# Norm affine and modulation applied to turned rows, bare normalised rows gathered, router by strips, opening reordered

## Chip, cores and metric

One core of a Trainium2 chip. The metric is device microseconds (us) of one execution of the whole program; lower is better. A core has TensorE (PE; its weight loads are listed as PEld), VectorE (DVE), ScalarE (ACT), GpSimd (POOL), SyncE (SP) and 16 DMA engines. The engines run their own instruction lists and meet at semaphores. A row of the trace names the line of the kernel that wrote the instruction.

## What is computed

A two-layer encoder in float32, 256 tokens of 1024 features, one conditioning vector c. Every sub-layer is modulated by vectors that come from c (`w_ada`), and closed by a layer norm with gain and offset:

```python
x = layer_norm(ALPHA * x + (1 + g1) * y, ln_mix_g[l], ln_mix_b[l])
h = x * (1 + sc2) + sh2
y = grouped_moe(h, router_w, router_b, w_gate[l], w_up[l], w_down[l])
x = layer_norm(ALPHA * x + (1 + g2) * y, ln_ffn_g[l], ln_ffn_b[l])
```

Layer 0's mixer is a causal convolution of 31 taps between two projections, layer 1's an attention with a forget gate (its keys and values have a modulation of their own, `w_ada_kv`). `grouped_moe` takes a softmax over 16 experts for each token, picks the best of four groups by the sum of its two best, and gives the token to those two experts.

## The kernel before

Tokens lie on the partitions in two tiles of 128 (`xs` for x, `hs` for h or for y). A product contracts over partitions, so h is turned: `turn_h` (L792) makes 16 transposes into PSUM banks 0 to 3, and `copy_hT` copies the banks to `hT` (ACT two, L552, DVE two, L1213).

Vectors that act along features are rows. `spread_row` (L767) multiplies a row by ones, which fills two PSUM banks with copies of it; DVE then combines all of `xs` with them. A close (`close_sublayer`) scales y by the gate row (L1271), adds it to x (L1275), takes mean and variance (L1280, L1283), normalises (L1288), multiplies by the gain row and adds the offset row (L1235, four operations). `modulate` does the same with scale and shift into `hs` (L1253, L1258); it also puts the features in the order in which the weights lie, a stride of four floats. PE spreads one row after another as DVE lets the banks go (`norm_spreads`), and between them computes the next part of `c @ w_ada` (`ada`, L742; the operand is c copied 32 times, `crep`), which DVE adds to its bias (`add_ada`, L1221).

`moe`: PE computes the router's logits with `hT` as the stationary operand (L852), DVE ranks experts and groups in small linked steps (L1299 to L1301), PE counts tokens, DVE builds places. Then for each expert and each block of 32 slots: DVE builds a 0/1 matrix G; PE gathers token rows of `hs` with it (`sum_x`, L885) and turns them (`turn_x`, L895); DVE copies them to `XT` (`take_xT`, L1389); PE multiplies by gate and up weights (`strips`, L904), DVE multiplies the two (L1399), PE turns that; DVE builds the weighting matrix (L1381, L1385), PE turns it (L922), combines the block before (L932) and multiplies by the down weights. An expert with several blocks runs the hidden part for all of them, then the result part. `zero_sums` (L858) clears four banks by a product, since results are added there.

Weights come in loads of 2 MB into a ring of eight slots (SP, L399), each load waiting until PE has used what its slot held; in the experts the slots are passed on by POOL (L511), and a ninth slot opens when the logits are done. Small rows go by ACT's and POOL's queues: x, then `b_ada`, then the rows of the convolution (`colrows`, L536).

In the opening PE takes two pieces of `w_ada`, turns `colrows` (L985), spreads taps (L993), takes two more pieces, spreads two rows, turns h and runs the first projection (L1011). The taps run on DVE (L1480) and PE (L1040); then come the convolution's norm over partitions (L1054, L1495, L1060) and the second projection (L808).

## Time and profile before

| | us |
|---|---|
| median of 3 runs | 1455.3 (1451.65 to 1455.41) |
| profiled execution | 1454.18 |
| its span | 1452.4 |
| PE busy | 1157.3 (80%) |
| DVE busy | 411.1 (28%) |
| ACT busy | 170.9 (12%) |
| chain that ended last | PE 56%, DMA 31%, DVE 8%, ACT 2% |

The stages of the profiled execution: the opening to 52.8, layer 0's mixer to 179.7, its close and the router to 234.4, its experts to 706.5, a close to 729, keys, values and attention to 902, a close and the router to 952, the second layer's experts to 1434, the last close and the output to the end. Shares of busy time are averages over stages with different limits; what a change is worth in a stage is read from what ends the waits there, and from when a load may be issued. The strips of the page cut the span in 40 slices of 36.3 us.

### The profile page before, as it was taken

To read this page: it belongs to the slowest core of one execution; us is meant where nothing else is said; L and a number is where in the kernel's file an instruction comes from. 1 tells how busy PE (TensorE), PEld (TensorE's weight loads), DVE (VectorE), ACT (ScalarE), POOL (GpSimd) and SP (SyncE) were. 2 spreads that over 40 slices of the span, in tenths; PEclk is the share of its full clock that TensorE was granted. 3 is DMA by queue.
4 is the path that set the end of the run, shared out by engine and by line. 5 is a ranking of instruction groups with operands and counts; after the bars stand their busy time and mean duration, and the time that the engine had idled before them with its cause. 6 is when DMAs were issued, how large, how long until landed. Compare 5 with 4: busy or idle time off the path is not lost.

```text
span 1452.4 us, 30514 instructions
## 1 busy us (share of the span) xinstructions
PE 1157.3 (80%) x13016; PEld 662.2 (46%) x13016; DVE 411.1 (28%) x1293; ACT 170.9 (12%) x415; POOL 21.4 (1%) x58
## 2 busy tenths in 40 slices
PE   2799978767998669867789989787689997697675
PEld 1685444433555335433374763444255553354342
DVE  0597063111222112111621331622122222121115
ACT  0003110000111001000100331010011110010001
POOL 3100000000000000000000000000000000000000
PEclk7899968888999899989879999678899998899887
DMA  9809859999999999999964022769999689999980
GB/s 374 358 20 421 357 245 398 425 425 426 366 395 410 426 427 425 422 424 424 416 273 151 24 117 92 313 268 426 423 425 396 279 353 426 427 425 422 424 347 30
DMA packets 49282, 494.70 MB, mean 341 GB/s; under 512 B 4231, under 2 KB 4247, under 8 KB 8988
## 3 DMA queue, kind: packets, MB, share of 16 engines
q1 hardware_dynamic: 48176, 490.75, 81.3%
q10 hardware_dynamic: 684, 2.32, 0.4%
q8 instruction: 77, 1.26, 0.3%
q0 software_dynamic: 320, 0.16, 0.1%
q14 instruction: 25, 0.20, 0.0%
HBM read 492.17 MB, written 1.05 MB: 340 GB/s over the span
## 4 chain that ended last, share of the span: by engine, by line
PE 56%; DMA 31%; DVE 8%; ACT 2%; issue 2%; ACTq 0%; DVEq 0%; POOL 0%; POOLq 0%
PE PS L904 25%; DMA ring<-in_w_up_dram 17%; DMA ring<-in_w_gate_dram 13%; PE PS L808 6%; PE PS L1011 4%; PE PS L932 3%; PE PS L742 3%; PE PS L885 2%; PE PS L826 2%; PE PS L1111 2%; DMA work<-in_conv_ln_b_dram 2%; DVE work L1381 1%; PE PS L895 1%; DVE xs L1235 1%; PE PS L792 1%
## 5 line engine op out<-in xcount | busy, mean ns | idle before, releaser
L904 PE MATMUL PS<-ring,work 128*32 128x256 f32 x8064 | 524.3, 417 | 114.6 <-DMA ring<-in_w_gate_dram 53.0
L904 PEld LDWEIGHTS PS<-ring,work 128*32 128x32 f32 x8064 | 280.2, 119 | 349.0 <-issue 110.5
L1399 DVE TENSOR_TENSOR work<-work,PS 128x256 f32<-128x256 f32 x47 | 19.8, 421 | 540.1 <-PE PS L904 540.1
L808 PE MATMUL PS<-ring,work 128*128 128x512 f32 x192 | 83.1, 593 | 0.5 <-ACT work L695 0.5
L742 PE MATMUL PS<-ring,crep 128*32 128x512 f32 x448 | 60.0, 689 | 19.7 <-DVE crep L1445 11.3
L932 PE MATMUL PS<-work 32*128 32x256 f32 x784 | 73.1, 499 | 3.1 <-ACT work L599 1.0
L904 PE MATMUL PS<-work 128*32 128x256 f32 x960 | 63.2, 408 | 15.4 <-DMA work<-in_w_up_dram 15.4
L922 PE MATMUL PS<-ident,work 128*128 128x128 f32 x94 | 22.9, 329 | 64.1 <-DVE work L1385 64.1
L1480 DVE SCALAR_TENSOR_TENSOR work<-work,colv 128x256 f32<-128x256 f32 x150 | 64.2, 486 | 1.2
L885 PE MATMUL PS<-hs,work 128*32 128x256 f32 x784 | 56.3, 406 | 3.8 <-DVE work L1372 3.8
L808 PEld LDWEIGHTS PS<-ring,work 128*128 128x128 f32 x192 | 36.3, 190 | 46.1 <-issue 45.3
L1410 DVE COPY work<-PS 128x256 f32<-128x256 f32 x47 | 20.0, 425 | 129.2 <-PE PS L932 129.2
L1011 PE MATMUL PS<-work,ring 128*128 128x256 f32 x256 | 55.5, 379 | 0.8 <-DVE work L1213 0.8
L599 ACT ACTIVATE work<-PS 128x256 f32<-128x256 f32 x47 | 18.1, 384 | 322.8 <-PE PS L904 322.8
L585 ACT ACTIVATE work<-PS 128x256 f32<-128x256 f32 x49 | 18.8, 384 | 316.0 <-PE PS L885 316.0
L1381 DVE TENSOR_SCALAR work<-slots,late,share 128x128 f32<-128x128 f32 x188 | 52.3, 341 | 0.9 <-issue 0.9
L1011 PEld LDWEIGHTS PS<-work,ring 128*128 128x128 f32 x256 | 48.6, 190 | 7.6 <-DVE work L1213 1.0
L904 PEld LDWEIGHTS PS<-work 128*32 128x32 f32 x960 | 32.6, 116 | 41.5 <-DMA work<-in_w_up_dram 19.3
L932 PEld LDWEIGHTS PS<-work 32*128 32x128 f32 x784 | 43.4, 225 | 17.5 <-ACT work L599 7.7
L589 ACT ACTIVATE work<-PS 128x256 f32<-128x256 f32 x47 | 18.1, 384 | 240.9 <-PE PS L904 240.9
L922 PEld LDWEIGHTS PS<-ident,work 128*128 128x128 f32 x94 | 10.2, 152 | 77.9 <-DVE work L1385 71.7
L742 PEld LDWEIGHTS PS<-ring,crep 128*32 128x32 f32 x448 | 15.6, 123 | 58.4 <-issue 46.0
(220 smaller groups left out, 884.9 us busy)
## 6 DMA issues: line engine op xcount, KB each, us to landing
ring<-in_w_gate_dram SPq DMA_DIRECT2D x64, 2048.0 KB, 26.2
ring<-in_w_up_dram SPq DMA_DIRECT2D x54, 2048.0 KB, 26.2
ring<-in_w_down_dram SPq DMA_DIRECT2D x54, 2048.0 KB, 27.9
ring<-in_w_ada_dram SPq DMA_DIRECT2D x24, 2048.0 KB, 18.8
work<-in_w_up_dram SPq DMA_DIRECT2D x10, 2048.0 KB, 23.9
work<-in_w_down_dram SPq DMA_DIRECT2D x10, 2048.0 KB, 27.4
ring<-in_w_pw_dram SPq DMA_DIRECT2D x6, 2048.0 KB, 38.8
ring<-in_w_ada_kv_dram SPq DMA_DIRECT2D x4, 2048.0 KB, 15.1
```

Of the source, the lines that this page charges most:

```text
L742: last = pe.matmul(PS[32 * q:32 * q + 32, bank, :], crep[:, k, :], quarter(index + j, kk, 2)[:, q * BANK:(q + 1) * BANK], start=(k == 0), ...
L808: last = pe.matmul(PS[:, banks + 2 * t + q, :], rows[:, k, t * P:(t + 1) * P], quarter(index + h, kk, KH)[:, q * BANK:(q + 1) * BANK], sta ...
L826: last = pe.matmul(PS[:, banks + f // 2, (f % 2) * SEQ:(f % 2 + 1) * SEQ], quarter(index + h, kk, KH)[:, f * P:(f + 1) * P], hT[:, k, :], ...
L885: last = pe.matmul(X_ps[SLOTS * q:SLOTS * (q + 1), :], G[:, t, :], hs[:, t, q * QUART:(q + 1) * QUART], start=(t == 0), stop=(t == TT - 1) ...
L904: last = pe.matmul(dst[SLOTS * s:SLOTS * (s + 1), :], rows[:, cc, SLOTS * q:SLOTS * (q + 1)], quarter(load + h, kk, KH)[:, QUART * s:QUART ...
L922: last = pe.transpose(GWT_ps[:, t * P:(t + 1) * P], GW[0][:, t, :, :].rearrange("p r s -> p (r s)"), ident[:, :])
L932: last = pe.matmul(sums(t, s), GWT[SLOTS * s:SLOTS * (s + 1), t * P:(t + 1) * P], yb[SLOTS * s:SLOTS * (s + 1), :], start=False, stop=(clo ...
L1011: last = pe.matmul(PS[:, f, g * SEQ:(g + 1) * SEQ], quarter(L_PW1 + j, kk, 2)[:, g * D + f * P:g * D + (f + 1) * P], hT[:, k, :], start=(k ...
L1111: last = pe.matmul(PS[:, (i + 1) % 2, SEQ:2 * SEQ], quarter(L_WQ + k // KH, k % KH, KH)[:, i * P:(i + 1) * P], hT[:, k, :], start=(k == 0) ...
L1381: last = dve.tensor_scalar(GW[i][:, t, :, :], every, late[i][:, t:t + 1], share[i][:, t:t + 1], ALU.is_equal, ALU.mult)
L1410: dve.tensor_copy(GWT, GWT_ps).then_inc(GWT_copied, 1)
L1480: ins = dve.scalar_tensor_tensor(out=CV[:, fc, :], in0=U[:, fc, j:j + SEQ], scalar=colv[:, fc, j:j + 1], in1=CV[:, fc, :], op0=ALU.mult, o ...
```

## The change

Vectors along features become columns: `columns` multiplies the rows that hold a modulation by a few columns of the identity, so that each feature's value stands on its partition (`mcol`); the norm vectors are turned once in the opening (`lncol`). `affine` on POOL combines gain, offset, scale and shift to one pair of columns a stage (`acol`): n*g*s and b*s + t. After a close only n = (x - mean) * rstd is made, into `hs`, one tile on DVE and one on ACT; it is turned, and `copy_hT` applies the pair. `sum_x` gathers rows of n, and `take_xT` applies the pair to the gathered tokens. x itself (n*g + b) is made later by `keep_x`, during the first expert or the key projection. The logits are computed with `rw` as the stationary operand, four products abreast in strips of 32 partitions, the strips then summed by a second small product. The ranking compares all pairs at once. ACT clears the sums. c is broadcast instead of copied. In the opening x is turned before its modulation is known, small rows are issued in another order, and the columns of the convolution are turned and the taps spread later.

PE's list in the opening, from the last of the spread taps on (the rows ahead are L742 x16, L985 and the rest of L993), before:

```order
L993 MATMUL PS<-colv,ident 32x8x7
L742 MATMUL PS<-ring,crep 32x512 x16
L767 MATMUL PS<-modv,ones 128x512 x4
L792 MATMUL PS<-ident,hs 128x128 x16
L1011 MATMUL PS<-work,ring 128x256 x128
```

and after, from its start:

```order
L826 MATMUL PS<-ring,cact 32x512 x8
L886 MATMUL PS<-ident,xs 128x128 x16
L826 MATMUL PS<-ring,cact 32x512 x24
L862 MATMUL PS<-ident,modv 128x4 x4
L1090 MATMUL PS<-ident,work 128x36 x8
L1094 MATMUL PS<-ident,work 128x8 x8
L1117 MATMUL PS<-work,ring 128x256 x32
```

The turning (L792, now L886) moved from behind all of `w_ada` to behind its first piece; the projection (L1011, now L1117) follows the turned columns, and its first two eighths stand ahead of the taps.

PE's list from the last product of layer 0's mixer to the first counting product, before:

```order
L1070 MATMUL PS<-work,ones 128x512 x4
L767 MATMUL PS<-modv,ones 128x512 x2
L742 MATMUL PS<-ring,crep 32x512 x32
L767 MATMUL PS<-lnrows,ones 128x512 x4
L767 MATMUL PS<-modv,ones 128x512 x4
L792 MATMUL PS<-ident,hs 128x128 x16
L852 MATMUL PS<-rw,work 128x16 x16
L742 MATMUL PS<-ring,crep 32x512 x16
L868 MATMUL PS<-r_sel,before 128x16
```

and after:

```order
L1176 MATMUL PS<-work,ones 128x512 x4
L851 MATMUL PS<-modv,ones 128x512 x2
L862 MATMUL PS<-ident,modv 128x4 x8
L826 MATMUL PS<-ring,cact 32x512 x32
L886 MATMUL PS<-ident,hs 128x128 x16
L945 MATMUL PS<-work,rw 32x256 x8
L953 MATMUL PS<-lane,work 128x16 x4
L851 MATMUL PS<-lnrows,ones 128x512 x4
L826 MATMUL PS<-ring,cact 32x512 x16
L965 MATMUL PS<-r_sel,before 128x16
```

The broadcasts of `lnrows` went from ahead of the turning to behind the logits, those of `modv` before it gave way to eight products for columns, and the logits are 8 + 4 products for 16.

DVE's list in the loop over an expert's blocks, from the building of G (L1368 and L1372) on, before:

```order
L1368 TENSOR_SCALAR work<-slots,place 128x32 x2
L1370 REGISTER_ALU
L1372 SCALAR_TENSOR_TENSOR work<-slots,place,work 128x32 x2
L1399 TENSOR_TENSOR work<-work,PS 128x256
L1389 COPY work<-PS 128x256
```

and after:

```order
L1481 TENSOR_SCALAR work<-slots,place 128x32 x2
L1483 REGISTER_ALU
L1485 SCALAR_TENSOR_TENSOR work<-slots,place,work 128x32 x2
L1517 TENSOR_TENSOR work<-work,PS 128x256
L1505 TENSOR_TENSOR work<-PS,acol 128x256
L1507 TENSOR_TENSOR work<-work,acol 128x256
```

The copy of the gathered tokens became two operations.

The core of the diff:

```diff
             def load(index, source):
                 if index in opens:
-                    sp.wait_ge(logits_done, opens[index] + 1)
+                    sp.wait_ge(logits_parted, 2 * opens[index] + 2)
...
+            def affine(to, gain, offset, scale, shift):
+                pool.tensor_tensor(acol[:, to, 0, :], lncol[:, :, gain], mcol[:, scale[0], scale[1], :], ALU.mult).then_inc(acol_part, 1)
+                pool.tensor_tensor(acol[:, to, 1, :], lncol[:, :, offset], mcol[:, scale[0], scale[1], :], ALU.mult).then_inc(acol_part, 1)
+                parts_made[0] += 2
+                pool.wait_ge(acol_part, parts_made[0])
+                pool.tensor_tensor(acol[:, to, 1, :], acol[:, to, 1, :], mcol[:, shift[0], shift[1], :], ALU.add).then_inc(acol_ready, 1)
+            pool.wait_ge(lncol_copied, 1)
+            pool.wait_ge(col_copied, 2)
+            affine(OF_FFN0, MIX_G, MIX_B, (2, 0), (1, 1))
...
-            act.wait_ge(mods_zeroed, 3)
-            load_bias(modv[0], b_ada[0], 3, mod0_in)
...
+            act.wait_ge(mods_zeroed, 3)
+            load_bias(modv[0], b_ada[0], 3, mod0_in)
...
+            for r, w in ((MIX_G, ln_mix_g), (MIX_B, ln_mix_b), (FFN_G, ln_ffn_g), (FFN_B, ln_ffn_b)):
+                act.dma_start(brow[32 + r:32 + r + DEPTH, :], w).then_inc(lnr_in, 16)
...
+            def copy_hT(scale, shift, ready=None):
+                if ready is not None:
+                    act.wait_ge(acol_ready, ready)
                 for b in (0, 2):
                     act.wait_ge(h_turned, 4 * turned[0] + b + 1)
-                    act.activation(hT[:, 2 * b:2 * b + 2, :], PS[:, b, :].rearrange("p (k t) -> p k t", k=2),
-                                   ACT.Copy).then_inc(hT_copied, 1)
+                    for k in (2 * b, 2 * b + 1):
+                        last = act.activation(hT[:, k, :], PS[:, b, (k % 2) * SEQ:(k % 2 + 1) * SEQ], ACT.Identity,
+                                              bias=shift[:, k:k + 1], scale=scale[:, k:k + 1])
+                    last.then_inc(hT_copied, 1)
...
+                if norms[0] < 2 * TT * DEPTH:
+                    act.wait_ge(shift_ready, norms[0] // TT)
+                    act.activation(chunks(hs, 1), by_chunk(xs[:, 1, :]), ACT.Identity, bias=negm[:, 0:1],
+                                   scale=rstd[:, 1:2]).then_inc(n_half, 1)
...
+                for b in range(4):
+                    act.activation(PS[:, b, :], ones[:, 0:1].to_broadcast([P, BANK]), ACT.Copy,
+                                   scale=0.0).then_inc(sums_zeroed, 1)
...
+            def spread_mod(tile, v, bank):
...
+            def turn_n(norms):
+                pe.wait_ge(h_ready, norms)
+                pe.wait_ge(n_half, norms)
+                turn_h(lambda t, k: hs[:, t, k * P:(k + 1) * P])
...
+            def moe(index, l):
+                h_there()
+                for kk in range(2):
+                    for q in range(4):
+                        last = pe.matmul(PS[32 * q:32 * q + 32, (B_GATE, B_M)[kk], 0:SEQ],
+                                         rw[:, 2 * q:2 * q + 2, :].rearrange("p k e -> p (k e)"), hT[:, 2 * q + kk, :],
+                                         start=True, stop=True, tile_position=(0, 32 * q), skip_group_check=True)
+                    last.then_inc(logits_parted, 1)
+                pe.wait_ge(parts_kept, l + 1)
+                pe.wait_ge(parts_copied, l + 1)
+                for t in range(TT):
+                    for kk in range(2):
+                        last = pe.matmul(PS[:, B_UP, 2 * E + t * E:2 * E + (t + 1) * E],
+                                         parts[:, kk, t * P:(t + 1) * P], lane[:, kk * E:(kk + 1) * E],
+                                         start=(kk == 0), stop=(kk == 1))
+                last.then_inc(logits_done, 1)
                 pe.wait_ge(rows_in[l], ROWS)
-                spread_ln(2 * which)
-                spread_ln(2 * which + 1)
...
-                for t in range(TT):
-                    for k in range(KD):
-                        last = pe.matmul(PS[:, B_GATE, t * E:(t + 1) * E], hT[:, k, t * P:(t + 1) * P],
-                                         rw[:, k, :], start=(k == 0), stop=(k == KD - 1))
-                last.then_inc(logits_done, 1)
...
-                    for b in range(4):
-                        behind(pe.matmul(PS[:, b, :], ident[0:1, 1:2].to_broadcast([1, P]), hs[0:1, 0, 0:BANK],
-                                         start=True, stop=False, skip_group_check=True))
...
+                    if e == 0:
+                        pe.wait_ge(sums_zeroed, 4 * (l + 1))
...
+            pe.wait_ge(c_acted, 1)
+            ada_load(L_ADA0_G0, 0, 4)
             pe.wait_ge(consts, CONSTS)
-            pe.wait_ge(c_spread, 1)
-            ada_load(L_ADA0_G0, 0, 0)
-            ada_load(L_ADA0_G0, 1, 0)
+            pe.wait_ge(x_in, 16 * TT)
+            turn_h(lambda t, k: by_chunk(xs[:, t, :])[:, k // KH, k % KH, :])
+            for j in range(1, ADA_G):
+                ada_load(L_ADA0_G0, j, 4)
+            pe.wait_ge(ada_added, 1)
+            columns(5, ((modv[0], 0),))
...
+            pe.wait_ge(lnr_in, 16 * 4)
+            for k in range(KD):
+                last = pe.matmul(PS[:, 6, 384 + 8 * k:392 + 8 * k], by_chunk(brow[32:40, :])[:, k // KH, k % KH, :],
+                                 ident[32:40, 32:40], start=True, stop=True, tile_position=(32, 0), skip_group_check=True)
...
-            ada_load(L_ADA0_G0, 2, 0)
-            ada_load(L_ADA0_G0, 3, 0)
-            pe.wait_ge(ada_added, 1)
-            spread_mod(modv[0], 1)
-            spread_mod(modv[0], 0)
-            pe.wait_ge(taps_copied, 3)
-            turn_h()
...
+            h_there()
             for f in range(KD):
+                if f == 2:
+                    pe.wait_ge(cols_copied, 1)
+                    pe.wait_ge(lncol_copied, 1)
+                    for q in range(4):
+                        for s in range(4):
+                            of_shift = colv[:, :, s:TAPS:4]
+                            last = pe.matmul(PS[32 * s:32 * s + 32, 7, 64 * q:64 * (q + 1)].rearrange("p (k m) -> p k m", k=KD)[:, :, 0:of_shift.shape[2]],
+                                             ident[:, 32 * q:32 * q + 32], of_shift, start=True, stop=True,
+                                             tile_position=(0, 32 * s), skip_group_check=True)
...
             pe.wait_ge(ada_added, 3)
-            norm_spreads(0, 0, L_ADAKV)
+            spread_mod(modv[0], 2, 4)
+            columns(7, ((modv[0], 1), (modv[0], 2)))
+            ada(L_ADAKV, 6)
+            turn_n(1)
             pe.wait_ge(ada_added, 4)
-            spread_mod(modv[0], 4)
-            spread_mod(modv[0], 3)
-            turn_h()
             moe(L_MOE0, 0)
...
-            spread_mod(modkv, 1)
...
-            pe.wait_ge(ada_added, 6)
-            turn_h()
-            spread_mod(modv[1], 1)
-            spread_mod(modv[1], 0)
-            project_T(L_WK, 0, k_done)
-            pe.wait_ge(spread_used, SPREADS0 + 4)
+            spread_mod(modv[0], 5, 4)
+            columns(7, ((modkv, 0), (modv[1], 0)))
+            ada(L_ADA1_G1, 6)
+            turn_n(2)
+            h_there()
...
+                pe.wait_ge(ada_added, 6)
+                spread_ln(2, 6)
+                spread_ln(3, 4)
+            project_T(L_WK, 0, k_done, between=(ffn_rows,))
+            pe.wait_ge(spread_used, SPREADS0)
             project(L_WV, 4, v_done)
...
-            norm_spreads(1, 0, L_ADA1_G2)
+            spread_mod(modv[1], 2, 4)
+            ada(L_ADA1_G2, 6)
             pe.wait_ge(ada_added, 7)
-            spread_mod(modv[1], 4)
-            spread_mod(modv[1], 3)
-            turn_h()
+            columns(7, ((modv[1], 1), (modv[1], 2)))
+            turn_n(3)
             moe(L_MOE1, 1)
-            norm_spreads(1, 1)
+            spread_mod(modv[1], 5, 4)
...
+                if ready is not None:
+                    dve.wait_ge(acol_ready, ready)
                 for b in (1, 3):
                     dve.wait_ge(h_turned, 4 * turned[0] + b + 1)
-                    dve.tensor_copy(hT[:, 2 * b:2 * b + 2, :],
-                                    PS[:, b, :].rearrange("p (k t) -> p k t", k=2)).then_inc(hT_copied, 1)
+                    for k in (2 * b, 2 * b + 1):
+                        last = dve.tensor_scalar(hT[:, k, :], PS[:, b, (k % 2) * SEQ:(k % 2 + 1) * SEQ],
+                                                 scale[:, k:k + 1], shift[:, k:k + 1], ALU.mult, ALU.add)
+                    last.then_inc(hT_copied, 1)
...
+            def keep_x(banks):
+                x_of = lambda t: by_chunk(xs[:, t, :])
+                with_row(banks[0], x_of, lambda t: chunks(hs, t), ALU.mult)
+                with_row(banks[1], x_of, x_of, ALU.add)
...
+                if done is None:
+                    dve.scalar_tensor_tensor(out=negm[:, 0:1], in0=mv[:, 1, 0:1], scalar=-1.0, in1=rstd[:, 1:2],
+                                             op0=ALU.mult, op1=ALU.mult).then_inc(shift_ready, 1)
+                    dve.tensor_scalar(chunks(hs, 0), by_chunk(xs[:, 0, :]), mv[:, 0, 0:1], rstd[:, 0:1],
+                                      ALU.subtract, ALU.mult).then_inc(h_ready, 1)
+                    if ada_next is not None:
+                        add_ada(*ada_next, 6)
+                    return
...
+            def ranks(rank, values, rows):
+                n = values.shape[-1]
+                mine = values.unsqueeze(3).to_broadcast([P, rows, n, n])
+                others = values.unsqueeze(2).to_broadcast([P, rows, n, n])
+                dve.tensor_tensor(r_gt[:, 0:rows], others, mine, ALU.is_gt)
+                link(dve.tensor_tensor(r_ge[:, 0:rows], others, mine, ALU.is_ge))
+                link(dve.tensor_tensor(r_ge[:, 0:rows], r_ge[:, 0:rows],
+                                       lower[:, :, :].unsqueeze(1).to_broadcast([P, rows, n, n]), ALU.mult))
+                link(dve.tensor_tensor(r_ge[:, 0:rows], r_ge[:, 0:rows], r_gt[:, 0:rows], ALU.max))
+                link(dve.tensor_reduce(rank, r_ge[:, 0:rows], AX.X, ALU.add))
...
-                    dve.tensor_copy(XT.rearrange("p c s -> p (c s)"), XT_ps).then_inc(XT_copied, 1)
+                    to = XT.rearrange("p c (q s) -> p c q s", q=STRIPS)
+                    over = [acol[:, (OF_FFN0, OF_FFN1)[l], i, :].rearrange("p (q c) -> p c q", c=NC).unsqueeze(3).to_broadcast([P, NC, STRIPS, SLOTS])
+                            for i in range(2)]
+                    dve.tensor_tensor(to, XT_ps.rearrange("p (c q s) -> p c q s", c=NC, q=STRIPS), over[0], ALU.mult).then_inc(XT_begun, 1)
+                    dve.wait_ge(XT_begun, n + l)
+                    dve.tensor_tensor(to, to, over[1], ALU.add).then_inc(XT_copied, 1)
...
+                keep_x((0, 2))
...
-                dve.tensor_tensor(CV[:, k, :], CV[:, k, :], PS[:, 4, 0:SEQ], ALU.subtract).then_inc(cen_ready, 1)
+                dve.scalar_tensor_tensor(out=CV[:, k, :], in0=PS[:, 4, 0:SEQ], scalar=-1.0 / D, in1=CV[:, k, :],
+                                         op0=ALU.mult, op1=ALU.add).then_inc(cen_ready, 1)
```

## Rows read from the trace of the kernel before

**Rows 1.** The page: clock, DMA share and rate in 40 slices of the span.

```profile
PEclk7899968888999899989879999678899998899887
DMA  9809859999999999999964022769999689999980
GB/s 374 358 20 421 357 245 398 425 425 426 366 395 410 426 427 425 422 424 424 416 273 151 24 117 92 313 268 426 423 425 396 279 353 426 427 425 422 424 347 30
```

**Rows 2.** Timeline of the opening: start us, us, engine, line, operation [idle before].

```profile
8.92 0.27 ACTq L536 DMA_DIRECT2D work<-in_conv_ln_b_dram  x1
...
32.32 1.06 PE L985 MATMUL PS<-ident,work 36*128 36x36 f32 x8 [9.07 <-DMA work<-in_conv_ln_b_dram]
...
33.93 1.14 PE L993 MATMUL PS<-colv,ident 128*32 128x64 f32 x30 [0.55 <-DVE colv L1447]
...
52.77 55.52 PE L1011 MATMUL PS<-work,ring 128*128 128x256 f32 x256 [0.78 <-DVE work L1213]
```

**Rows 3.** Busy time by window in the opening; last three: clock, DMA share, GB/s.

```profile
72.00:74.00 2.00, 2.00 (x11) 1.77 (x10) 2.00 (x6) 0.21 (x1) 0.00 (x0) 1.00 0.08 33
74.00:76.00 2.00, 2.00 (x11) 1.74 (x10) 2.00 (x6) 0.27 (x1) 0.00 (x0) 1.00 0.00 0
```

**Rows 4.** Timeline from the first close to the first expert, columns as in rows 2.

```profile
189.09 1.54 DVE L1288 TENSOR_SCALAR xs<-xs,mv,rstd 128x1024 f32<-128x1024 f32 x2
...
196.96 3.84 DVE L1253 TENSOR_TENSOR hs<-xs,PS 128x1024 f32<-128x1024 f32 x2
...
200.83 2.35 DVE L1258 TENSOR_TENSOR hs<-hs,PS 128x1024 f32<-128x1024 f32 x2
...
203.24 3.67 PE L792 MATMUL PS<-ident,hs 128*128 128x128 f32 x16 [4.18 <-DVE hs L1258]
...
207.69 7.01 PE L852 MATMUL PS<-rw,work 128*128 128x16 f32 x32 [0.78 <-DVE work L1213]
...
218.34 2.45 SPq L399 DMA_DIRECT2D ring<-in_w_down_dram  x2
...
234.45 9.49 PE L904 MATMUL PS<-ring,work 128*32 128x256 f32 x128 [0.52 <-DVE work L1389]
```

**Rows 5.** Busy time by window, same stretch: clock, DMA share, GB/s last.

```profile
206.00:207.00 1.00, 0.91 (x5) 0.51 (x3) 0.05 (x1) 0.89 (x2) 0.00 (x0) 0.50 0.24 98
```

**Rows 6.** The chain that ended last, in order of time: start, us, what.

```profile
259.89 36.34 DMA ring<-in_w_gate_dram
...
347.81 7.11 PE PS L904 x128
```

**Rows 7.** Waits of TensorE, 342 to 465.3: total us, times, longest.

```profile
PE PS L922 <- DVE work L1385: 8.0, 4, 2.0
PE PS L904 <- DVE work L1389: 2.1, 4, 0.5
```

**Rows 8.** The same view, 1053 to 1192.4.

```profile
PE PS L904 <- DVE work L1389: 3.6, 5, 0.8
```

**Rows 9.** The page: a group of instructions, busy us, mean ns | idle before.

```profile
L1399 DVE TENSOR_TENSOR work<-work,PS 128x256 f32<-128x256 f32 x47 | 19.8, 421 | 540.1 <-PE PS L904 540.1
```

**Rows 10.** Timeline of the close after the first experts.

```profile
715.70 0.17 DVE L1286 RECIPROCAL rstd<-rstd 128x2 f32<-128x2 f32 x1 [0.47 <-ACT rstd L576]
...
729.27 3.64 PE L792 MATMUL PS<-ident,hs 128*128 128x128 f32 x16 [4.27 <-DVE hs L1258]
```

**Rows 11.** Busy time by window at the key projection: clock, DMA share, GB/s last.

```profile
740.00:741.00 1.00, 1.00 (x4) 0.73 (x4) 1.00 (x2) 0.00 (x0) 0.00 (x0) 0.50 1.01 401
```

**Rows 12.** Timeline from the close after attention to the second layer's experts.

```profile
911.41 0.17 DVE L1286 RECIPROCAL rstd<-rstd 128x2 f32<-128x2 f32 x1 [0.47 <-ACT rstd L576]
...
926.00 3.31 PE L792 MATMUL PS<-ident,hs 128*128 128x128 f32 x16 [4.18 <-DVE hs L1258]
...
948.33 1.94 PE L885 MATMUL PS<-hs,work 128*32 128x256 f32 x16 [3.77 <-DVE work L1372]
...
955.91 0.33 SPq L399 DMA_DIRECT2D ring<-in_w_up_dram  x1
```

270 lines of the change are left out of this document (145 added, 125 removed).

## The prediction

> **What bounds the kernel now.** I read the strips of the page first [rows 1]: the DMA strip is full (425 GB/s) from the seventh slice to the nineteenth and again from 27 to 36, with holes in the opening, ahead of the first expert and in attention. The full stretches are the experts' weights (2 MB a load, eight slots and a spare). So in the experts the stream of weights or TensorE is late, and outside them a chain through TensorE, VectorE and ScalarE. A microsecond taken from that chain counts if TensorE, or a load that waits for a slot, gets earlier by it. I therefore read each place twice: who ends the chain, and when the next load may be issued.
>
> **Opening.** TensorE waits 9 us for small rows until 32.32, and starts the big projection (L1011, 55.5 us) at 52.77 [rows 2]. The change issues the rows sooner, turns bare x, and drops two broadcasts and four wide VectorE steps from this chain. By the chain alone the projection could start some 8 us sooner. The weights speak against it. Something like one engine of sixteen is still busy in 72 to 74 (share 0.08), none in 74 to 76 [rows 3]: the last of the twelve loads issued by then lands at about 74 on a slow engine. A load is 2.1 MB, 131 KB an engine; at 425 GB/s for sixteen that is 4.93 us. Four loads follow the projection's, so its last piece lands by 74 - 4 x 4.93 = 54.3, and the old kernel wants it after six products of 0.434, at 55.4. It was just in time. The new kernel puts four small loads more (rows of the norm vectors) ahead of it: say 0.9 us, so 55.2. From there 122 of the 128 products remain (52.9 us), and the tap spreading, 1.14 us [rows 2], now stands inside the projection: its end is 109.3 for 108.3. **+1.0**, bounds -3.5 (the slow engine's piece lands at 50, and the projection starts when the small rows are in) and +9 (those rows, issued at about 14, land only at 61; the row that ended the old wait took from 8.92 to 32.3).
> The Trainium skill (DMA: Bandwidth & Descriptors, "Why a DMA increments its semaphore by 16 and not by 1") says that a transfer of one row, or of 31, runs on one engine, the lowest-numbered. The lone late engine of [rows 3] agrees. If rows were spread over all engines instead, the weights would be in at about 46 and the opening would give 8 us.
> Conv and its norm: eight subtractions become scalar_tensor_tensor, about 0.49 for 0.42 [rows 9], beside TensorE products of 0.43: **+0.3**, bounds 0 and +1.
>
> **First close and router.** The normalisation starts at 189.09. Until the turning at 203.24 the old chain has it, four row operations, two multiplications of strided x (3.84) and two additions (2.35) [rows 4]. The new chain has a 128x1 step (0.2) and one half on each of VectorE and ScalarE. The plain form costs 0.77 a half [rows 4]; its input now has a stride, and the strided multiplication costs 1.92 where the addition costs 1.18. I take 1.9, the nearer row. Turning starts at about 191.3, 12 sooner; TensorE's ada product no longer waits for y and has ended by then. [...]
> The copies do two operations for one: +0.2. Logits: 7.01 us for 32 small records [rows 4] become eight products four abreast (two groups at the experts' 0.44, a sixteenth of 7.11 [rows 6]), a copy of 0.42 and eight small records of 0.22: 3.3 with waits. So they come 15.3 us sooner. Ranking goes from 20 linked steps to 10 (-1.7), but hidden: TensorE now has two row broadcasts (2 to 4 us, by clock) ahead of the ada pieces.
> What that buys is read from the loads. The down weights were issued at 218.34, 3.6 us after the logits [rows 4], when the first ada piece gave up its slot; the engines had run dry at 206.3 [rows 5]. Now they are issued at 199.4 + 2..4 + 3.6 = 205 to 207, just as the engines run dry. The hole of 12 us closes. The experts' first product comes some 19 us sooner (234.45 before), but from 260 on it is the stream that decides [rows 6]. **-12.0**, bounds -9 (a quarter of the hole left) and -12.8. On ScalarE the zeroing of the sums waits for four row operations on VectorE (2 x 1.18 + 2 x 1.92 = 6.2, up to 7.7) and delays the first expert by 2 to 3 us: covered by those 7 us of lead.
>
> **In the experts.** Gain and offset are applied where gathered tokens are copied: two operations for one, +0.45 with the link. TensorE feels it twice: where the same expert has a further block it waits for that copy, and once an expert, since the matrix it waits 2.0 us for (L1385) is built behind it. In the TensorE-bound stretch of the first layer there are 4 and 4 such waits [rows 7], in the second's 5 [rows 8] and again 4 (its row reads as in rows 7). Elsewhere a gate load ends the wait. After the last loads of a layer come two such places. First layer (4 + 4 + 2) x 0.45 = **+4.5**, second (5 + 4 + 2) x 0.45 = **+4.9**; bounds 0, if loads hide all, and +14, if an operation takes 0.7 us rather than the 0.42 of its nearest relative [rows 9].
>
> **Second close.** From the reciprocal (ends 715.87) to the turning at 729.27 [rows 10] 13.4 us become 2.2: -11.2. Copies +0.2, the two broadcasts ahead of the key projection go (-2.1), two go into it (+1.8): -11.3 at the old clock. The clock still stood at its 1.2 GHz level (0.50) in 740 to 741 [rows 11], after a long wait; against 2.4 GHz that cost up to 1.8 us in the turning (half of its 3.6, [rows 10]) and 2.6 in the five microseconds of projection before 741. TensorE now waits only 2 us and may keep 2.4 GHz. I take half: **-13.5**, bounds -11 and -16. Later, the query's copies: **+0.4**.
>
> **Attention's close.** Here the new column products stand behind the ada addition, which VectorE does after its half. Reciprocal done 911.58, addition done 914.3, eight small products (1.8 to 3.5), turning at 916 to 917.5 for 926.00 [rows 12]: -9.3. Logits -1.5 with the copies, ranking -1.7: the first gathering at about 935.8 for 948.33, then +0.45 for the new step. The next load waited for the first expert's slot, until 955.91 [rows 12]. **-12.2**, bounds -9 and -14; no load hides it, since the engines are idle until that issue. The last close keeps its order: 0.
>
> **Sum**: 1.0 + 0.3 - 12.0 + 4.5 - 13.5 + 0.4 - 12.2 + 4.9 = -26.6. From the profiled execution, 1454.2, that gives 1427.6; it lay 1.1 below the median, so for the median 1455.3 - 26.6 = 1428.7, **1429**.
>
> **Rivals.** (1) The opening gives what its chain shows, the last weights landing near 46: 9 us better than my term, **1420**. For it: no load ends a wait at 52.77. Against: the lone engine. 0.12. (2) The norm rows hold the projection until 61: 8 more, **1437**. For: 23 us for one row. Against: most of that queue's bytes, the 31 tap rows, now go first. 0.10. (3) Loads hide the extra operation: 9.4 less, **1419**. 0.08. (4) TensorE's waits of 2.0 us grow to 2.45 and its clock drops more often (+3), and half the router's hole stays open (+6): **1438**. 0.10. (5) Slower: two operations with broadcast column pairs take so long that 21 places on the path eat the gains. Without the expert terms the sum is -36; over 21 places that is 1.7 us each, so the pair must take 2.1 us instead of my 0.87, or 1.07 an operation. At 1.35 an operation the kernel ends at 1419.3 + 21 x 2.3 = **1468**. Against: 0.42 in the nearest row. 0.02. (6) The change doesn't do what it says: the row operations only move and the first experts lose what the first and third close win, +24, **1453**. Against: the first expert's products alone last 9.49 us [rows 4]. 0.03.
>
> **How the numbers follow.** My case has 0.55, its own range 1422 to 1436. With most of (1) to (4) the range is **1418 to 1438**; (5), (6) and the tails stay out. A measurement of this kernel tells about 0.3%, 4.4 us, from no change. Faster 0.95 (all but 5 and 6), same 0.03 (case 6), slower 0.02.
>
> **What would show it.** The projection from about 51 to 109; turnings some 12, 11 and 9 us sooner after their reciprocals; no DMA hole before the first down load; two VectorE operations of 0.42 at the gathered copy and TensorE's 2.0 us wait at 2.45; the second layer's first gathering 12 us sooner in its stage. I am wrong if the projection starts by 46, if a close's turning waits for columns, or if the first expert's delay exceeds its lead.

## The result, and the profile after

| | before | after |
|---|---|---|
| median | 1454.6 us (6 runs) | 1443.4 us (6 runs, 1440.4 to 1445.7) |
| ratio | | 0.9926, 95% interval 0.9902 to 0.9950 |
| profiled execution | 1454.2 | 1440.4 |
| PE busy | 1157.3 | 1147.8 |
| ACT busy | 170.9 | 188.0 |

The change gains 11.2 us on the medians and 13.8 between the two profiled executions (the one of after is its lowest run), where I had forecast 26.6 from a median. It is faster, as forecast, and by less than half as much.

The strips of the page of after (columns as in [rows 1]):

```profile
PEclk7799989889999989987899989688799998899897
DMA  9809869999899999999994021889998689999990
GB/s 376 363 3 404 356 249 423 424 427 425 370 369 402 422 425 426 424 424 424 416 382 155 21 118 59 350 330 424 423 426 353 265 364 425 426 426 422 424 380 29
```

The holes of the opening and of attention are there as before. In the sixth slice (180 to 216 us), where I expected the hole to close, stands 249 GB/s for 245.

I cut both executions at the same places and took the differences of the lengths:

| stretch, and the mark at its end | before | after | forecast | measured |
|---|---|---|---|---|
| opening, convolution and its norm: second projection starts | 148.32 | 157.21 | +1.3 | +8.9 |
| first close, router: the gate load issued at 284 | 284.25 | 283.75 | -12.0 | -9.4 |
| first experts: last combining product ends | 706.39 | 711.68 | +4.5 | +5.8 |
| second close, keys: value projection starts | 766.08 | 758.17 | -13.5 | -13.2 |
| attention: output projection starts | 874.47 | 870.29 | +0.4 | +3.7 |
| third close, router: next load issued | 955.91 | 941.68 | -12.2 | -10.0 |
| second experts: last combining product ends | 1433.36 | 1419.59 | +4.9 | +0.5 |

The stretches sum to -13.8. The largest miss is the first line, and this profile flatters it: six variants below have the opening of after unchanged, and in their profiles the second projection starts at 159.0 to 163.2. The profile of after, at 157.2, is the earliest of the seven. The middle one (159.6) would make the first line +11.3, which would account for most of the 2.6 us by which the medians gain less than the two profiled executions.

**The opening.** Timeline of after (start us, us, engine, line, operation, idle before), TensorE, then ScalarE, then VectorE:

```profile
45.10 3.90 PE L1094 MATMUL PS<-ident,work 8*128 8x8 f32 x16 [3.07 <-DMA work<-in_ln_ffn_b_dram]
48.93 5.49 PE L1117 MATMUL PS<-work,ring 128*128 128x256 f32 x12
56.23 11.49 PE L1117 MATMUL PS<-work,ring 128*128 128x256 f32 x52 [1.81 <-DMA ring<-in_w_pw_dram]
67.65 1.14 PE L1105 MATMUL PS<-colv,ident 128*32 128x64 f32 x32
68.72 41.71 PE L1117 MATMUL PS<-work,ring 128*128 128x256 f32 x192
...
133.15 5.26 PE L1146 MATMUL PS<-work,hs 128*32 128x256 f32 x64 [3.07 <-POOL hs L523]
141.76 3.72 PE L1160 MATMUL PS<-work,ones 128*128 128x256 f32 x16 [3.36 <-DVE work L1590]
157.21 27.73 PE L909 MATMUL PS<-ring,work 128*128 128x512 f32 x64
```
```profile
68.86 0.36 ACT L698 ACTIVATE work<-PS 128x224 f32<-128x224 f32 x1 [19.30 <-PE PS L1105]
...
70.64 0.84 ACT L707 ACTIVATE work<-PS,colv 128x256 f32<-128x256 f32 x2
```
```profile
71.22 0.49 DVE L1573 SCALAR_TENSOR_TENSOR work<-PS,colv,work 128x256 f32<-128x256 f32 x1 [28.01 <-ACT work L707]
...
123.15 18.55 DVE L1590 SCALAR_TENSOR_TENSOR work<-work,colv 128x256 f32<-128x256 f32 x38
```

The projection starts at 48.93, as its chain allows, and waits at 56.23 for its last weights: the price of the norm rows that I had estimated (0.9, landing at 55.2) was about right. It ends at 110.4. But now the mean's product (L1160) no longer follows TensorE's own work: it waits 3.36 us for a VectorE tap operation. VectorE works almost without a gap from 71.2 to 141.7, and the run starts 10.7 us later than before. The reason stands two rows up: ScalarE's copies of the spread taps (L698) stand ahead of its first sigmoid (L707) and wait for the spreading, which now lies behind a quarter of the projection.

A second engine is late too. The wait ahead of the row at 133.15 is for GpSimd, whose four products for the last stack of taps took 8.19 us for 3.02 in the kernel before, beside VectorE at work:

```profile
124.90 8.19 POOL L523 TENSOR_TENSOR hs<-lane,work 128x256 f32<-128x256 f32 x4 [50.39 <-PE PS L1146]
```

TensorE's last convolution products end at 138.4 by it (132.2 before). VectorE ends later still, so VectorE is what the mean's product waits for.

### The profile page after: what moved, and what is told of

Read it like the earlier page. It is cut to its first block, busy times and chain, and to the rows that moved or that the text cites. A ratio compares the mean times of both kernels' runs of the same rounds, so it can differ in the third digit from the quotient of the medians.

```text
span 1438.7 us, 30568 instructions
## 1 busy us (share of the span) xinstructions
PE 1147.8 (80%) x13016; PEld 664.3 (46%) x13016; DVE 410.7 (29%) x1310; ACT 188.0 (13%) x446; POOL 30.4 (2%) x67
## 4 chain that ended last, share of the span: by engine, by line
PE 52%; DMA 30%; DVE 13%; ACT 2%; issue 2%; SPq 0%; DVEq 0%; ACTq 0%; POOLq 0%
PE PS L1002 26%; DMA ring<-in_w_up_dram 17%; DMA ring<-in_w_gate_dram 9%; PE PS L909 6%; DVE work L1590 4%; PE PS L1030 4%; DMA ring<-in_w_pw_dram 3%; PE PS L981 2%; PE PS L1221 2%; PE PS L826 2%; PE PS L927 2%; DVE work L1494 1%; DVE xs L1350 1%; PE PS L993 1%; DVE work L1505 1%
## 5 line engine op out<-in xcount | busy, mean ns | idle before, releaser
L826 PE MATMUL PS<-ring,cact 128*32 128x512 f32 x448 | 61.8, 706 | 21.2 <-DMA ring<-in_w_ada_dram 21.2
L1002 PE MATMUL PS<-work 128*32 128x256 f32 x960 | 62.1, 402 | 12.2 <-DMA work<-in_w_up_dram 12.2
L1117 PE MATMUL PS<-work,ring 128*128 128x256 f32 x256 | 58.7, 392 | 1.8 <-DMA ring<-in_w_pw_dram 1.8
L1117 PEld LDWEIGHTS PS<-work,ring 128*128 128x128 f32 x256 | 50.1, 197 | 9.9 <-DMA ring<-in_w_pw_dram 2.5
L826 PEld LDWEIGHTS PS<-ring,cact 128*32 128x32 f32 x448 | 14.9, 124 | 61.2 <-issue 48.2
## 6 DMA issues: line engine op xcount, KB each, us to landing
ring<-in_w_gate_dram SPq DMA_DIRECT2D x64, 2048.0 KB, 26.6
```

What stands on the lines that cost most here:

```text
L826: last = pe.matmul(PS[32 * q:32 * q + 32, bank, :], cact[:, k:k + 1].to_broadcast([P, 32]), quarter(index + j, kk, 2)[:, q * BANK:(q + 1) ...
L1002: last = pe.matmul(dst[SLOTS * s:SLOTS * (s + 1), :], rows[:, cc, SLOTS * q:SLOTS * (q + 1)], quarter(load + h, kk, KH)[:, QUART * s:QUART ...
L1117: last = pe.matmul(PS[:, f, g * SEQ:(g + 1) * SEQ], quarter(L_PW1 + j, kk, 2)[:, g * D + f * P:g * D + (f + 1) * P], hT[:, k, :], start=(k ...
```

## Experiments: where the opening went

The times beside an experiment are medians. The kernel before ran beside each on the same chip, at a median of 1451.4 to 1453.8, and the ratio is to that.

**The part alone, in the kernel before.** The 16 spreading products moved into the first projection (to bank 7), their copies to ScalarE ahead of the sigmoids:

```diff
             for f in range(KD):
+                if f == 2:
+                    pe.wait_ge(cols_copied, 1)
...
+                    last.then_inc(taps_spread, 1)
...
+            act.wait_ge(taps_spread, 1)
+            act.activation(taps4[:, :, :, 0:FOURS - 1], spread4[:, :, :, 0:FOURS - 1], ACT.Copy).then_inc(taps_copied, 1)
             for f in range(KD):
                 act.wait_ge(u_mm, f + 1)
```

> The kernel before with one part of the change alone: the tap spreading stands inside the first projection, ahead of its third eighth, and ScalarE copies the spread taps ahead of its sigmoids. The rest is the kernel before. Theory A (VectorE's run of tap operations is what ends the mixer): the run starts at about 71 instead of 60.6, and the kernel gets 7 to 10 us slower (0.5 to 0.7%). Theory B, which my prediction held: 1.1 us of products more inside the projection, 1 us slower or nothing.

Measured: 1460.1 against 1452.5, ratio 1.0053 (1.0035 to 1.0071), 7.5 us slower. The timeline of VectorE, and of TensorE at the mean:

```profile
70.38 0.48 DVE L1466 SCALAR_TENSOR_TENSOR work<-PS,colv,work 128x256 f32<-128x256 f32 x1 [17.63 <-ACT work L628]
```
```profile
140.88 5.66 PE L1061 MATMUL PS<-work,ones_d 128*128 128x256 f32 x16 [4.95 <-DVE work L1483]
```

This one step of the change accounts for the loss in the opening: the run starts 9.8 us late, the mean's product comes at 140.9 for 132.9, and the second projection starts at 158.25 for 148.32. Of these 9.9 us 1.9 are the mean's product at the clock's lower level (5.66 for 3.72, behind a wait of 4.95). GpSimd's last four products took 8.14 here as well.

**ScalarE's copies behind two sigmoids, in the changed kernel.**

```diff
-            act.wait_ge(taps_spread, 1)
-            act.activation(taps4[:, :, :, 0:FOURS - 1], spread4[:, :, :, 0:FOURS - 1], ACT.Copy).then_inc(taps_copied, 1)
...
             for f in range(KD):
+                if f == 2:
+                    act.wait_ge(taps_spread, 1)
+                    act.activation(taps4[:, :, :, 0:FOURS - 1], spread4[:, :, :, 0:FOURS - 1], ACT.Copy).then_inc(taps_copied, 1)
                 act.wait_ge(u_mm, f + 1)
```

> The changed kernel with one edit: ScalarE copies the spread taps after the first two sigmoids of the gated unit instead of ahead of them; TensorE's list is untouched. In the changed kernel those copies wait until 68.9 us, VectorE's run of tap operations starts at 71.2 (60.6 before) and ends at 142.4, which ends the wait of the mean's product at 141.8. Theory A (that run is the bound of the mixer, and the copies ahead of the sigmoids start it late): it starts at about 62, the mean's product comes at about 134, and the kernel ends some 7 to 9 us sooner than the changed one, about 19 us under the kernel before. Theory B (the bound is the projection's end at 110.4 or the stacks of taps on GpSimd, which need the same copies): VectorE starts sooner but the mean's product stays within 2 us of 141.8, and the whole gains under 2 us.

Measured: 1432.4, ratio 0.9874 (0.9841 to 0.9907), 20.1 under the kernel before. The run starts at 64.6 for the 62 expected, and the mean's product comes at 136.9 for 134. Part of it is GpSimd's stack of taps, here with VectorE in the same time:

```profile
71.35 5.85 POOL L523 TENSOR_TENSOR hs<-lane,work 128x256 f32<-128x256 f32 x8 [58.11 <-ACT work L703]
```
```profile
72.11 8.93 DVE L1591 SCALAR_TENSOR_TENSOR work<-work,colv 128x256 f32<-128x256 f32 x16
```

The same sixteen operations last 6.42 us elsewhere, 0.40 each for 0.56 on the mean here. But TensorE was late as well. It did the first products behind its last weights partly at 1.2 GHz (the 52 records up to the spreading took 13.18 us for 11.49 in the profile of after), its projection ended at 112.2, and its last convolution product at 136.24, only 0.6 ahead of VectorE. So the slow operations alone do not explain the 136.9.

**Another order of the opening.** The taps spread at f == 0, the norm rows loaded behind the second sigmoid and turned behind the last convolution product:

```diff
-                if f == 2:
+                if f == 0:
                     pe.wait_ge(cols_copied, 1)
-                    pe.wait_ge(lncol_copied, 1)
...
             conv_fours(len(CONV_PE) - 1)
+            pe.wait_ge(lnr_in, 16 * 4)
+            for k in range(KD):
...
+            last.then_inc(cols_turned, 1)
```

> The changed kernel with its opening put in another order: the taps are spread ahead of the first projection (in the time in which TensorE waits for its last weights, 56.2 us), the four small loads of norm rows are issued after the second sigmoid instead of at 11.4, and their rows are turned after the last convolution product. Where the tap copies alone were moved, VectorE's run started at 64.6 and slowed from 0.40 to 0.56 us an operation while GpSimd built its stack of taps (71.4 to 77.2), and the projection ended at 112.2. Theory: without the four loads the weights land sooner (54 to 55 instead of 56.4), the spreading leaves the projection (-1.1), the stack is built before VectorE's run. Projection's end 108.5 to 110.5, run from 61 to 63 with no slow operations, mean's product at 133 to 135 (136.9 with the copies alone moved), kernel 1 to 4 us under that one. Rival: GpSimd's stack was not what slowed VectorE: slow operations at the same place of the run, mean's product at 136 or later.

Measured: 1437.3, ratio 0.9902 (0.9872 to 0.9932). By its ratio it lies between the changed kernel (0.9926) and the run before it (0.9874), with an interval that overlaps both, and the mean's product came at 138.6. VectorE, TensorE, and the clock (third column from the end) of this kernel:

```profile
71.69 6.41 DVE L1592 SCALAR_TENSOR_TENSOR work<-work,colv 128x256 f32<-128x256 f32 x16
```
```profile
55.20 55.71 PE L1114 MATMUL PS<-work,ring 128*128 128x256 f32 x244 [3.14 <-DMA ring<-in_w_pw_dram]
134.78 3.90 PE L1156 MATMUL PS<-ident,work 8*128 8x8 f32 x16
```
```profile
56.00:58.00 2.00, 2.00 (x6) 1.55 (x6) 0.00 (x0) 0.00 (x0) 0.00 (x0) 0.50 1.03 430
```

With the stack built at 45.6 to 50.3 the sixteen operations take 6.41 us again: GpSimd had slowed VectorE. The norm rows cost the weights 1 us (55.20 for 56.23), as forecast. But that bought nothing here: TensorE had waited 7.1 us from 42 to 56 (4.9 in after) and did the first products at its 1.2 GHz level (0.50). This order is not needed for it, though: of the nine profiles of the changed kernel and its variants in which the spreading stands at f == 2, six had it too (13.2 to 14.5 us for the 52 records ahead of the spreading, for 11.5). And the turned rows, hidden in the opening, now stood on TensorE's path (3.9 us). This run is a miss of my own design; the expected end of 133 to 135 left out both.

**The spreading alone ahead of the projection.** One line of the changed kernel:

```diff
-                if f == 2:
+                if f == 0:
                     pe.wait_ge(cols_copied, 1)
```

> The changed kernel with one line moved: the taps are spread ahead of the first projection instead of ahead of its third eighth. GpSimd's stack is then built ahead of VectorE's run of tap operations, ScalarE's copies stand ahead of its first sigmoid but wait for nothing, and the spreading falls into the wait for the last weights (to 56.2). VectorE's run from about 64.5 with no slow operations to 134, projection's end 110.8 to 111.2, mean's product at 135.5 (141.8 in the changed kernel). Kernel 6 to 9 us under the changed one, at about 1435.

Measured: 1431.4, ratio 0.9851 (0.9828 to 0.9874), 11 us under the changed kernel by the ratios (0.9926 there), 8.2 by the spans of the two profiles, where 6 to 9 were expected. Its opening:

```profile
49.64 1.16 PE L1105 MATMUL PS<-colv,ident 128*32 128x64 f32 x32 [0.71 <-ACT lncol L694]
...
56.14 52.93 PE L1117 MATMUL PS<-work,ring 128*128 128x256 f32 x244 [1.37 <-DMA ring<-in_w_pw_dram]
...
133.67 3.72 PE L1160 MATMUL PS<-work,ones 128*128 128x256 f32 x16 [0.65 <-ACT work L719]
...
149.12 11.43 PE L909 MATMUL PS<-ring,work 128*128 128x512 f32 x26
```

The projection ends at 109.1 and the second one starts at 149.1, 0.8 after the kernel before, where I had forecast +1.3 for the opening. The version below, with the same opening, has 149.2. From there nearly every mark of the program, up to the last, lies 8.1 to 8.2 us ahead of the changed kernel's (5 to 10 in parts of the first experts). The opening's miss is the place of the spreading, and it counts in full at the end.

## Experiments: the first close and the router

**Columns behind the ada product.** In after, TensorE and SyncE (first gate loads):

```profile
191.02 3.90 PE L862 MATMUL PS<-ident,modv 128*128 128x4 f32 x16
194.84 8.55 PE L826 MATMUL PS<-ring,cact 128*32 128x512 f32 x64
203.33 1.97 PE L886 MATMUL PS<-ident,hs 128*128 128x128 f32 x16
```
```profile
198.31 2.06 SPq L425 DMA_DIRECT2D ring<-in_w_gate_dram  x2
```
```profile
194.00:196.00 2.00, 2.00 (x12) 1.22 (x16) 1.97 (x3) 1.03 (x2) 0.68 (x2) 0.50 0.00 0
```

No idle time stands in the three rows: TensorE itself is now the bound of the close, at the clock's lower level (0.50), while the normalised rows were ready at 201.9 (VectorE's half takes 1.26 us, ScalarE's 2.32). And the ada product, whose pieces free the slots, stands 3.9 us further back, so the engines are idle (share 0.00) from 192 to 198. One hole closed (206 to 219), another opened.

```diff
-            columns(7, ((modv[0], 1), (modv[0], 2)))
             ada(L_ADAKV, 6)
+            columns(7, ((modv[0], 1), (modv[0], 2)))
...
-            columns(7, ((modkv, 0), (modv[1], 0)))
             ada(L_ADA1_G1, 6)
+            columns(7, ((modkv, 0), (modv[1], 0)))
```

> The changed kernel with the column products of the first and the second close behind the ada product instead of ahead of it (and ScalarE's copy of the columns behind its half of the normalised rows). In the changed kernel the ada product of the first close starts at 194.8, behind two broadcast products and 3.9 us of column products, and the first gate load is issued at 198.3, when its first piece has given up a slot; the DMA engines are idle from 191 to 198. Theory A (the slots set the stream, and the columns hold them): gate issue at about 194.5, the stream of the first experts 4 us sooner, the last of layer 0's loads as well, kernel some 3 to 4 us under the changed one. Theory B (TensorE is the bound of the first close: columns and ada product last 12.5 us in any order, turning at 203.3 as it is): the gate loads come sooner, but nothing in the experts does, 0 to 1 us.

Measured: 1442.1, ratio 0.9933 (0.9908 to 0.9958), the same as the changed kernel. The gate loads are issued at 194.81 and the turning comes at 203.58, although this profile's second projection had started 1.8 us later. The clock stayed low through the router:

```profile
207.00:209.00 2.00, 1.59 (x16) 0.68 (x16) 0.26 (x1) 0.44 (x2) 0.00 (x0) 0.50 1.05 451
```

where the changed kernel has

```profile
207.00:209.00 2.00, 1.37 (x19) 0.91 (x11) 0.42 (x1) 1.67 (x2) 0.00 (x0) 1.00 0.95 410
```

The first gathering came at 226.3 for 222.2. The lead of the loads was lost again on the way: the first down load has to wait for a piece of the ada product behind the logits, was issued at 218.85 for 214.54, and the engines were nearly idle (share 0.06 and 0.21) from 216 to 220. The last combining product of layer 0 ends at 711.68 in both. So theory B holds for the whole.

**Both edits.**

> Both edits, the tap copies behind two sigmoids and the ada product ahead of the columns. If both theories A hold the two gains add: 11 to 13 us under the changed kernel, 22 to 25 under the kernel before. If the stream of loads has hidden one by the other, less than 9.

Measured: 1434.9, ratio 0.9867 (0.9843 to 0.9892): the gain of the tap copies alone (0.9874), nothing added. This run also answers what earlier loads are worth at an equal clock. Beside the run with the tap copies alone it has the same opening (second projection at 152.2 for 152.4) and nearly the same low clock in the router. Its gate loads were issued 4.5 us sooner (188.96 for 193.47), its first down load 2.1 later (214.72 for 212.65), behind a second hole:

```profile
212.00:214.00 2.00, 2.00 (x16) 0.45 (x12) 1.64 (x10) 0.00 (x0) 0.00 (x0) 0.50 0.00 0
```

Layer 0's last combining product ended at 707.5 for 707.1: the earlier gate loads were worth nothing.

**The old logits in the changed kernel.**

```diff
-                for kk in range(2):
-                    for q in range(4):
-                        last = pe.matmul(PS[32 * q:32 * q + 32, (B_GATE, B_M)[kk], 0:SEQ],
...
+                for t in range(TT):
+                    for k in range(KD):
+                        last = pe.matmul(PS[:, B_UP, 2 * E + t * E:2 * E + (t + 1) * E], hT[:, k, t * P:(t + 1) * P],
+                                         rw[:, k, :], start=(k == 0), stop=(k == KD - 1))
```

> The changed kernel with the logits of the kernel before (16 products with the turned tokens as the stationary operand) in place of the strips and their sum. It prices the router part. From the turning to the first broadcast after the logits 5.9 us pass now; with 32 small records of 0.16 to 0.22 it is 8.5 to 10. Layer 0: the first gathering 3 to 4 us later, but from 284 us on nothing, since the stream of loads decides. Layer 1: the next load after the first expert's slot 3 to 4 us later, and the end as well. Sum 3 to 4 us slower than the changed kernel; if layer 0 counts too, 6 to 8.

Measured: 1443.0, ratio 0.9967 (0.9925 to 1.0009); beside 1443.4, no difference that the medians show. Two of its seven runs lie at 1451.7 and 1459.2, and the interval leaves room for the 3 to 4 us expected. In its profile the first gathering came at 228.4 for 222.2 (2.0 of it from ahead of the close), and layer 0 ended 0.2 us later than in the changed kernel: the stream of loads took all of it. In layer 1 the turning and the gathering lie 23.1 us apart for 20.5, so there the strips are worth 2.6.

## Experiments: the second operation at the gathered tokens

The two waits of TensorE that it touches, 342 to 470 us of after (total us, times, longest; of before see [rows 7]):

```profile
PE PS L1020 <- DVE work L1498: 9.9, 4, 2.5
PE PS L1002 <- DVE work L1507: 3.9, 4, 1.0
```

2.5 for 2.0 and 1.0 for 0.5, four of each: the mechanism and the size per place are as forecast. What is in question is how many places count. In the whole of layer 0 there are 16 and 8 of these waits, in layer 1 16 and 9, where my sum had 10 and 11 in all.

```diff
-                    dve.tensor_tensor(to, XT_ps.rearrange("p (c q s) -> p c q s", c=NC, q=STRIPS), over[0], ALU.mult).then_inc(XT_begun, 1)
-                    dve.wait_ge(XT_begun, n + l)
-                    dve.tensor_tensor(to, to, over[1], ALU.add).then_inc(XT_copied, 1)
+                    dve.tensor_copy(XT.rearrange("p c s -> p (c s)"), XT_ps).then_inc(XT_copied, 1)
```

> The changed kernel with one operation in place of two where the gathered, turned tokens are copied: gain, offset and modulation are left out there, so the experts get bare normalised rows (the router still has them). It prices the second operation in the experts. By the prediction's terms 4.5 + 4.9 = 9.4 us faster than the changed kernel, 4 to 5 in each layer. Rival A: the stream of loads hides it in layer 1 (its experts came out only 0.4 us longer than before): 5 us in layer 0, 0 to 1 in layer 1. Rival B: the experts' 5.8 us in layer 0 are the stream, which had caught up with its lead: under 3 us in all.

> The changed kernel with a third operation there (the offset columns are added twice), the same cost as the change's second operation once more. If each counts at 21 places of 0.45 us: 9 to 10 us slower than the changed kernel, 4 to 5 in each layer, and as much as leaving the second operation out gives. If some are hidden by loads now and no more with a longer chain, more than that; if TensorE's clock holds the sum up, less.

Measured: 1431.0 for one operation and 1434.5 for three, both faster than the changed kernel. Neither can be read as a price: the values that they leave out or add change the second layer's routing. The product of gate and up was run 48 times in the first and 46 in the second, for 47 ([rows 9] and after):

```profile
L1515 DVE TENSOR_TENSOR work<-work,PS 128x256 f32<-128x256 f32 x48 | 20.2, 421 | 523.6 <-PE PS L1002 519.8
```
```profile
L1519 DVE TENSOR_TENSOR work<-work,PS 128x256 f32<-128x256 f32 x46 | 19.4, 421 | 493.1 <-PE PS L1002 489.3
```

In layer 0, where the routing is the same, one operation fewer can be set beside the run with the old logits, which has the same starts within 1.3 us: its layer 0 ended at 705.5 against 711.9, 6.4 us for one operation (at a mean clock of 0.98 against 0.95 from 345 to 470, so not all of it is the operation).

So I added operations that change no value:

```diff
-                    dve.tensor_tensor(to, to, over[1], ALU.add).then_inc(XT_copied, 1)
+                    dve.tensor_tensor(to, to, over[1], ALU.add).then_inc(XT_begun, 1)
...
+                    dve.tensor_tensor(to, to, to, ALU.max).then_inc(XT_begun, 1)
...
+                    dve.tensor_tensor(to, to, to, ALU.max).then_inc(XT_copied, 1)
```

> The changed kernel with two further operations at the copy of the gathered tokens, each the maximum of the copy with itself, so no value changes and every expert has the blocks of the changed kernel (leaving an operation out had moved the routing of the second layer). Four operations in place of two: 0.92 us more at 21 places are 19 us, 9.2 in layer 0 and 10.1 in layer 1, if each counts as my prediction held; half of that (9 to 10) is then the price of the change's own second operation. If loads hide it where a stretch is followed by a full stream: 5 to 12 us.

> The changed kernel with one further operation at the copy of the gathered tokens (the maximum of the copy with itself; no value changes). Two further ones cost 28.5 us on the medians, 10.2 in layer 0 and 20.1 in layer 1, which is more than twice the change's own second operation (by the traces 5 to 6 in layer 0, 0.4 in layer 1). If every operation beyond the second counts alike: 13 to 15 us slower than the changed kernel, about 1457, 5 in layer 0 and 9 to 10 in layer 1. If loads still hide part of the third: 6 to 10, and the fourth carries the rest.

> The kernel before with one operation more at that copy (the maximum of the copy with itself), and nothing else of the change. It prices the step from one operation to two with layer 1's routing unchanged. By my prediction's terms 4.5 + 4.9 = 9.4 us slower. By the two traces of before and after, 5.3 to 5.8 in layer 0 and 0.4 in layer 1: 6. If the second layer's 0.4 was TensorE's clock at the end of the one profile of before (last strips at 3.64 us for 1.93), 7 to 9.

| operations at the copy | kernel | median | step | layer 0, profile | layer 1, profile |
|---|---|---|---|---|---|
| 1 to 2 | before, one more | 1463.8 for 1453.8 | +10.0 | +5.9 | +0.1 |
| 2 to 3 | after, one more | 1454.1 for 1443.4 | +10.7 | +0.4 | +12.0 |
| 2 to 4 | after, two more | 1471.9 for 1443.4 | +28.5 | +10.2 | +20.1 |

(The shift against the kernel without the operations, at layer 0's last combining product less that ahead of its first gathering, and at layer 1's less that ahead of its own. The ratios to the kernel before are 1.0076 (1.0058 to 1.0094), 1.0003 (0.9990 to 1.0015) and 1.0135 (1.0114 to 1.0155).) By the medians the change's second operation costs 10.0 us (8.4 to 13.7 by the interval of the ratio), where I had forecast 9.4. The profiles don't place it so: of the 7.9 us between the two profiled executions 5.9 fall in the first experts, 0.1 in the second, and the rest in the opening and the second close, where nothing was changed. With four operations the price per operation rises. The waits of TensorE in layer 0 (225 to 720 us) show part of why: in after and with two more,

```profile
PE PS L1020 <- DVE work L1498: 39.6, 16, 2.6
```
```profile
PE PS L1020 <- DVE work L1498: 54.6, 16, 3.8
```

From the first gathering to the last combining product all waits for VectorE grow from 50.9 to 71.8 us, and all waits for DMA fall from 63.7 to 40.7. As long as TensorE waits for loads anyhow, a longer VectorE step is paid from that, here in full. The +10.2 of layer 0 is TensorE's own work, which took 12 us more (the stretch less all waits), at a mean clock of 0.86 for 0.90. In layer 1 the waits for VectorE grow by 23.4, those for DMA fall by 11.9, and TensorE's work takes 8.6 more (0.87 for 0.89). So a dearer fourth operation is in the main a matter of the clock.

The same count for the first step, in layer 1 of the kernel before with one more: 11.6 us more of waits for VectorE, 8.1 less for DMA, and 3.4 less of TensorE's work, which is what leaves 0.1. In the profile of the kernel before some of the last strips of that layer ran at 3.64 us for 1.93, with the clock down, so a part of the 0.1 is luck of that profile. The +0.5 of the changed kernel is not luck of its own profile. From its first gathering to its last combining product the second layer took 486.0 us there, 485.7 to 486.1 in five other profiles of variants with two operations at the copy, and 482.1 and 487.7 in two more. The kernel before took 485.0, and 482.4 with the late taps. What puts the profile of after 3 us under its median is more likely its opening (see the table of stretches).

## Experiment: the third close, and the fastest version

In after the 16 column products wait for the ada addition and hold the turning:

```profile
909.40 3.90 PE L862 MATMUL PS<-ident,modv 128*128 128x4 f32 x16 [3.32 <-DVE modv L1338]
913.16 3.65 PE L886 MATMUL PS<-ident,hs 128*128 128x128 f32 x16
917.90 1.94 PE L945 MATMUL PS<-work,rw 128*32 128x256 f32 x16 [1.09 <-DVE work L1329]
920.48 1.86 PE L953 MATMUL PS<-lane,work 128*128 128x16 f32 x8 [0.64 <-DVE work L1419]
```

```diff
+            columns(7, ((modv[1], 1),), whole=False)
             pe.wait_ge(ada_added, 7)
-            columns(7, ((modv[1], 1), (modv[1], 2)))
+            columns(7, ((modv[1], 2),), first=1)
```

> As the run before, and in the close after attention the column product that needs no ada product stands ahead of the wait for it. In the changed kernel all 16 small products (3.9 us) stand behind that wait, from 909.4 to 913.2, and hold the turning. Turning some 1.8 us sooner, at 5.5 to 6.5 us after the reciprocal instead of 8; the second layer's experts and the end move with it, 1.5 to 2 us under the run before.

Measured: 1430.6, ratio 0.9845 (0.9819 to 0.9872), beside 1431.4 without this edit: the same within the noise. Its profile shows the mechanism:

```profile
900.51 2.03 PE L862 MATMUL PS<-ident,modv 128*128 128x4 f32 x8 [1.37 <-DVE modv L1340]
902.40 3.58 PE L887 MATMUL PS<-ident,hs 128*128 128x128 f32 x16
```

The turning comes 4.1 us after the reciprocal's start for 5.9 (the 8 in the expectation was misread; 5.9 is the changed kernel's value too), 1.8 sooner as expected, and the second layer's first gathering lies 3.9 us ahead of the run before (921.6 for 925.5), but at the end 1.8 to 2.1 are left. Both versions with the spreading ahead of the projection beat the two kernels: 1.5% under the kernel before, 0.8% under the changed one.

## Why the prediction was right or wrong, point by point

- **Opening, +1.3 forecast, +8.9 measured: the step that failed.** Projection and landing of the weights were right: last weights at 56.2 for 55.2, end at 110.4 for 109.3. I then priced the moved spreading as 1.14 us of TensorE inside the projection, and nothing of who waits for it. ScalarE's copies of the spread taps are queued ahead of its sigmoids, the sigmoids feed VectorE, and VectorE's run of tap operations goes from 60.6 to 130.8 in the kernel before, with one gap of 0.7 us. It ended 1.5 us ahead of TensorE's part there (132.2), and I had called only the projection's end the bound. Where two engines are that close, both have to be timed. The one-line experiment shows it: with the spreading ahead of the projection the second projection starts 0.8 us after the kernel before's, for the +1.3 forecast. That kernel measured 1431.4 where I had forecast 1429 for the changed one, though this nearness owes something to the misses below, which have both signs. The term for the convolution's norm (+0.3) was nothing: its eight operations took 2.74 us for 2.79.
- **First close and router, -12.0 forecast, -9.4 measured.** The half costs 1.26 on VectorE and 2.32 on ScalarE for my 1.9, fine; the hole before the down loads did close. But I had said that TensorE's ada product "has ended by then". It had not: broadcasts, columns and product fill TensorE until 203.3, 1.4 us past the rows' readiness, partly at 1.2 GHz. The sixteen records of column products (3.90 us) had no term in my sum for this close, and the slots behind them were freed 4 us later in relation to the stage. That is one of the signs of being wrong that I had named. The +8.9 of the opening and the -9.4 cancelled by chance, so at 284 us the changed kernel was level.
- **First experts, +4.5 forecast, +5.8 measured.** Right in mechanism and nearly in size, but with a wrong count: 2.0 became 2.5 sixteen times and 0.5 became 1.0 eight times, for the ten places of my sum. That is 11 us more of waiting in the kernel before with one more operation, of which loads gave back 4.9.
- **Second close, -13.5 forecast, -13.2 measured.** Right in the sum. The turning followed the ada product (8.95 us, for 7.07 at the full clock) instead of the rows, 4.0 us after the reciprocal's end for my 2.2: 1.8 lost. Turning and key projection then ran at 2.4 GHz (1.97 us for 3.64, and two halves of 14.08 for 30.53). That is 4.0 of the 4.4 us of which I had taken half: 1.8 won. The two misses cancel, so the sum is right by luck.
- **Attention, +0.4 forecast, +3.7 measured.** The copies took 0.6: the wait is 2.56 us for 1.94. The other 3.1 lie between it and the output projection, 75.1 us for 72.0, and half of them in the first query, 5.23 us for 3.72 in the kernel before, at the lower clock:

```profile
795.22 0.39 PE L1211 MATMUL PS<-ident,work 16*128 16x16 f32 x2 [2.56 <-DVE work L1329]
795.54 5.23 PE L1221 MATMUL PS<-work,ring 128*128 128x256 f32 x16
```
```profile
795.00:798.00 3.00, 2.78 (x8) 2.30 (x9) 0.62 (x3) 0.00 (x0) 0.00 (x0) 0.53 0.00 0
```

  It is tempting to blame the longer wait for the fall of the clock, but the kernel before with one more operation has it behind the old wait:

```profile
810.30 0.34 PE L1102 MATMUL PS<-ident,work 16*128 16x16 f32 x2 [1.94 <-DVE work L1214]
810.57 5.31 PE L1112 MATMUL PS<-work,ring 128*128 128x256 f32 x16
```

  The kernel before with the late taps has 5.34, and the changed kernel's variants 5.1 to 5.2 (one 6.6). The whole part lasts 72.0 in all three profiles of the kernel before and its variants. Of the twelve of the changed kernel and its variants eight have 75.0 to 75.1, three 71.8 to 71.9 and one 76.1. So most of the 3.1 goes with the changed kernel, but not always, and what brings it stays open.
- **Third close, -12.2 forecast, -10.0 measured.** The turning came 8.7 sooner for 9.3. (The terms of my sum give 12.0 to 12.1, not 12.2.) The logits gave nothing here: from turning to logits it is 9.2 us in both, where I had 1.5 less; it seems that the two new copies and links cost what the products save at the lower clock. With the old logits under the new copies it is 2.6 more, so the strips only pay for the copies.
- **Second experts, +4.9 forecast, +0.5 measured.** The waits for VectorE grew by 14 us, more than my eleven places, and the waits for DMA fell by 11. So in the profiles the loads hid nearly all of it, which I had given a chance of 0.08. The medians put the price of both layers at 10.0 and so leave about 4 us of it that no profile places. That my 9.4 agrees with them does not confirm its split into 4.5 and 4.9.
- **The rivals.** None of them was the one that came. The fourth (1438) came nearest in effect, with the clock and a hole left open, the third holds for the second layer as far as the profiles go, and the fifth's price was far off: the operation takes 0.42 us. What was missing was a rival in which the convolution's other engines are late.

## What to carry to other kernels

When a product is moved back in TensorE's list, follow its readers through every queue: the copy that waits for it stands ahead of other work on its engine, and what that work feeds may be a stretch with no slack at all. Before a term is written for a stage, list each engine that is full there and when its run starts, and not only the one whose end the profile names as the bound. Small jobs belong where an engine waits for a load anyhow, since a later place may lie on a path. And price a small repeated step by medians of a kernel with one more of it that changes no value; a single profile moves by several microseconds (the same opening took 157 to 163), and a step that changes values may change how much work follows. Before a slower row is put down to a longer wait ahead of it, look for the same row in the profiles of the other variants.

## What the runs showed of the hardware

- VectorE and GpSimd slow each other: sixteen tap operations took 8.93 us while GpSimd multiplied in SBUF and 6.41 when it had done so earlier, and GpSimd's eight took 5.85 for 4.6. In the changed kernel it cost VectorE about 1 us, with the copies alone moved 2.8. GpSimd's last four took 8.1 to 8.2 us in the eight profiles in which VectorE's run started at 70 us or later, and 3.0 to 3.1 in the seven in which it started by 65 and another part of it was going on beside them. The Trainium skill (SBUF — State Buffer, "SBUF: two separate sides") says that the two share a pair of ports, which an operation of VectorE with two inputs in SBUF locks against one of GpSimd that reads SBUF, and that the later one waits. The tap operations have two such inputs; the runs agree.
- TensorE's clock can't be told here from the wait ahead of it alone. In attention, with waits of 1.33 and 1.94 us and 2 us of work between them, the query behind them was done at 2.4 GHz in one profile (3.72 us) and partly at 1.2 GHz in two (5.31, 5.34); behind waits of 1.33 and 2.56 it took 5.1 to 5.2 in eleven. In the opening, behind waits of 1.8 to 3.0 us, the next 52 records of the projection took 11.5 us in three profiles and 13.2 to 14.5 in six.
- VectorE's half of the normalisation, whose input has a stride of four floats (its output none), took 1.26 us for 1024 elements, between the plain form (0.77) and my 1.9. With a broadcast operand an operation on 256 elements took 0.42, as long as a plain one.
